# Gate products of three branches: one matmul of 512 columns for both parts of x, their halves added on the VectorE

## The reference

```python
h = rms_norm(h_res, pre_norm_g[i])            # 16 meta rows + 256 rows
z = h @ w_in[i]                               # the last 4096 columns are gl
y_a = (pool_mixer(pv, ...) * silu(pg)) @ w_out_pool[i]      # pool
y_b = (mla_attention(...) * silu(mg)) @ w_out_mla[i]        # mla
y_c = (conformer_conv(cu, ...) * silu(cg)) @ w_out_conf[i]  # conf
y_d = (short_conv(sbcx, ...) * silu(sg)) @ w_out_sc[i]      # sc
gts = sigmoid(gl + gate_bias[i]).reshape(b_, l_, 4, D_MODEL)
m = gts[:, :, 0] * y_a + gts[:, :, 1] * y_b + gts[:, :, 2] * y_c + gts[:, :, 3] * y_d
h_res = h_res + rms_norm(m @ w_o[i], post_norm_g[i])
```

## Time and profile before

| | |
|---|---|
| median of 3 runs | 875.02 us |
| the profiled execution | 877.89 us, its span 876.2 us |
| TensorE, matmuls | 863.1 us busy (99%), 5932 matmuls |
| VectorE | 588.7 us busy (67%) |
| ScalarE | 426.8 us busy (49%) |
| GpSimd | 86.8 us busy (10%) |
| HBM | 174 GB/s over the span |

### The profile page before, as it was taken

How to read it: one execution, slowest core, us unless ns; L and a number is a source line. 1 busy time by engine, 2 the same in 40 slices (tenths; PEclk the granted TensorE clock), 3 DMA queues, 4 the chain that set the end, 5 groups by cost and what they waited for, 6 DMA issues and landing times.

```text
span 876.2 us, 14097 instructions
## 1 busy us (share of the span) xinstructions
PE 863.1 (99%) x5932; PEld 795.3 (91%) x5932; DVE 588.7 (67%) x844; ACT 426.8 (49%) x614; POOL 86.8 (10%) x85
## 2 busy tenths in 40 slices
PE   8999999999999999999999999999999999999996
PEld 7998999999888988879999988889988899999885
DVE  4999956688586674786555554587987765555545
ACT  5656454456654873435444443255563554444320
POOL 0250100122003221011000000021100200000000
PEclk8999999999999999999999999999999999999999
DMA  9963776663356752547656656477544766565631
GB/s 288 246 182 101 192 212 175 176 184 121 97 168 185 239 159 91 157 153 243 187 177 190 191 185 198 125 244 223 162 142 131 237 185 192 177 185 192 188 125 49
DMA packets 121976, 154.51 MB, mean 176 GB/s; under 512 B 11647, under 2 KB 98074, under 8 KB 121914
## 3 DMA queue, kind: packets, MB, share of 16 engines
q1 hardware_dynamic: 120042, 148.36, 56.3%
q0 software_dynamic: 1872, 5.26, 2.0%
HBM read 151.48 MB, written 1.05 MB: 174 GB/s over the span
## 4 chain that ended last, share of the span: by engine, by line
PE 92%; DVE 4%; DMA 2%; ACT 1%; issue 1%; SPq 0%; DVEq 0%
PE acc L594 26%; PE acc L595 25%; PE acc L596 25%; PE acc L678 2%; PE acc L681 2%; PE acc L679 2%; PE acc L632 1%; DMA staged<-in_ffn_w_gu 1%; PE misc L762 1%; DMA x<-in_x 1%; DVE y L2108 1%; PE misc L819 1%; PE misc L1016 1%; ACT w_hi L1221 1%; DVE w_lo L1645 1%
## 5 line engine op out<-in xcount | busy, mean ns | idle before, releaser
L1645 DVE TENSOR_TENSOR w_lo<-staged,w_hi 128x1024 fp32r<-128x1024 f32 (+1 forms) x274 | 332.0, 1232 | 157.4 <-ACT w_hi L1221 156.5
L594 PE MATMUL acc<-x_hi,w_hi 128*128 128x256 f32 (+2 forms) x1288 | 365.8, 284 | 0.0
L595 PE MATMUL acc<-x_lo,w_hi 128*128 128x256 f32 (+2 forms) x1288 | 363.8, 282 | 0.0
L596 PE MATMUL acc<-x_hi,w_lo 128*128 128x256 f32 (+2 forms) x1288 | 361.2, 280 | 0.0
L1221 ACT CAST w_hi<-staged 128x1024 fp32r<-128x1024 f32 (+1 forms) x274 | 277.8, 1044 | 85.7 <-DMA staged<-in_ffn_w_down 44.6
L596 PEld LDWEIGHTS acc<-x_hi,w_lo 128*128 128x128 f32 x1288 | 243.7, 189 | 0.0
L594 PEld LDWEIGHTS acc<-x_hi,w_hi 128*128 128x128 f32 x1288 | 241.6, 188 | 1.7 <-issue 1.0
L595 PEld LDWEIGHTS acc<-x_lo,w_hi 128*128 128x128 f32 x1288 | 242.1, 188 | 0.7 <-issue 0.2
L594 PE MATMUL acc<-w_hi,h_hi 128*128 128x512 f32 (+1 forms) x176 | 66.4, 377 | 0.0
L595 PE MATMUL acc<-w_lo,h_hi 128*128 128x512 f32 (+1 forms) x176 | 66.4, 377 | 0.0
L596 PE MATMUL acc<-w_hi,h_lo 128*128 128x512 f32 (+1 forms) x176 | 66.2, 376 | 0.0
(11 more groups left out here) (394 smaller groups left out, 1149.5 us busy)
## 6 DMA issues: line engine op xcount, KB each, us to landing
staged<-in_ffn_w_gu SPq DMA_DIRECT2D x88, 512.0 KB, 3.6
staged<-in_w_in SPq DMA_DIRECT2D x58, 512.0 KB, 3.9
staged<-in_ffn_w_down SPq DMA_DIRECT2D x44, 512.0 KB, 3.5
staged<-in_gla_w_in SPq DMA_DIRECT2D x24, 512.0 KB, 3.7
staged<-in_moba_w_in SPq DMA_DIRECT2D x24, 512.0 KB, 3.9
staged<-in_w_o SPq DMA_DIRECT2D x8, 512.0 KB, 3.8
staged<-in_gla_w_out SPq DMA_DIRECT2D x8, 512.0 KB, 3.8
staged<-in_moba_w_out SPq DMA_DIRECT2D x8, 512.0 KB, 3.7
```

Of the source, the lines that this page charges most:

```text
L594: pe.matmul(dst, st_hi, mv_hi, start=start, stop=False)
L595: pe.matmul(dst, st_hi, mv_lo, start=False, stop=False)
L596: return pe.matmul(dst, st_lo, mv_hi, start=False, stop=stop)
L1645: nc.vector.tensor_tensor(lo, raw, hi, ALU.subtract).then_inc(split, 1)
```

## The change

For the gates of sc, pool and conf the two parts of x now lie in one tensor, and one matmul multiplies the high weights by both (256 columns of `x_hi`, then 256 of `x_lo`) into the whole of a bank; the low weights by `x_hi` add to its first half, as before in a matmul of 256 columns. A slot has 8 matmuls of 512 columns and 8 of 256. The VectorE adds the two halves of each bank by a `tensor_reduce` over a view in which they are innermost, writes `gates`, and frees the pair. The ScalarE waits for that and takes the sigmoids in place in SBUF. `gate_out` waits for them on a new semaphore, `gated`. The gates of mla are computed as before.

```diff
-        x_hi = place("x_hi", [KC, KEYS], F32R)
-        x_lo = place("x_lo", [KC, KEYS], F32R)
+        x_parts = place("x_parts", [2, KC, KEYS], F32R)
+        x_hi, x_lo = x_parts[:, 0], x_parts[:, 1]
...
+            def wide_slot(sl, p, half):
+                ready(sl)
+                hi = w_hi[:, sl.ring(), :].rearrange("p (c n) -> p c n", c=4)
+                lo = w_lo[:, sl.ring(), :].rearrange("p (c n) -> p c n", c=4)
+                for b in range(2):
+                    for c in range(4):
+                        k = half * 4 + c
+                        cols = slice(b * P, b * P + P)
+                        def with_both():
+                            return pe.matmul(acc[:, p, b, :].rearrange("p (s n) -> p s n", s=2), hi[:, c, cols],
+                                             x_parts[:, :, k, META:KEYS], start=k == 0, stop=k == KC - 1)
+                        def with_high():
+                            return pe.matmul(acc[:, p, b, 0:ROWS], lo[:, c, cols], x_hi[:, k, META:KEYS], start=False, stop=False)
+                        if k == 0:
+                            with_both()
+                            mm = with_high()
+                        else:
+                            with_high()
+                            mm = with_both()
+                mm.then_inc(weights_used, 1)
...
-            t_stage(FIRST["gate_sc"], 8, OUT["gate_sc0"], xm_hi, xm_lo)
+            wide_stage(FIRST["gate_sc"], 8, OUT["gate_sc0"])
...
-                t_stage(FIRST["gate_pool%d" % h], 4, OUT["gate_pool%d" % (2 * h)], xm_hi, xm_lo)
+                wide_gates("pool", h)
...
-                t_stage(FIRST["gate_conf%d" % h], 4, OUT["gate_conf%d" % (2 * h)], xm_hi, xm_lo)
+                wide_gates("conf", h)
...
             def take_gates(b, before, i):
-                name = "gate_%s%d" % (b, i)
-                if before:
-                    await_out(act, "y_%s%d" % (before, i))
-                nc.scalar.activation(gates[:, 2 * i, :], acc[:, pair(name), 0, 0:ROWS], ACT.Sigmoid,
-                                     bias=gate_bias(b, 2 * i))
-                copy_out(gates[:, 2 * i + 1, :], acc[:, pair(name), 1, 0:ROWS], name, ACT.Sigmoid,
-                         bias=gate_bias(b, 2 * i + 1))
+                await_out(act, "gate_%s%d" % (b, i))
+                for c in (2 * i, 2 * i + 1):
+                    last = nc.scalar.activation(gates[:, c, :], gates[:, c, :], ACT.Sigmoid, bias=gate_bias(b, c))
+                last.then_inc(s["gated"], 1)
...
             def gate_out(b, i):
                 name = "y_%s%d" % (b, i)
+                if b != "mla":
+                    dve.wait_ge(s["gated"], 4 * ("sc", "pool", "conf").index(b) + i + 1)
...
+            def gate_sum(stage, index):
+                name = ...
+                slot_done(dve, stage, index)
+                parts = acc[:, pair(name), :, :].rearrange("p b (s n) -> p b n s", s=2)
+                taken(nc.vector.tensor_reduce(halves(gates, int(name[-1])), parts, AX.X, ALU.add), name)
             for sl in slots(FIRST["gate_sc"], 8):
                 lead(sl)
+                if sl.index % 2 == 1:
+                    gate_sum("gate_sc", sl.index)
...
                     for sl in slots(FIRST[stage], 4):
                         lead(sl)
+                        if sl.index % 2 == 1:
+                            gate_sum(stage, sl.index)
```

More of the change, by code:

```diff
@@ L396, in hybrid_stack @@
             "cleared", "conf_rounded", "conf_sig", "conf_split", "conf_squared", "conf_u", "conf_zn", "const_loaded",
-            "conv_done", "cum_ready", "e_ready", "end_ready", "exp_done", "gain_loaded", "gain_scaled", "gg0_ready",
+            "conv_done", "cum_ready", "e_ready", "end_ready", "exp_done", "gain_loaded", "gated", "gain_scaled", "gg0_ready",
             "gg1_ready", "gk_loaded", "glu_ready", "h_rounded", "h_split", "half_ready", "heads_done", "intra_ready",
@@ L619, in t_stage, with wide_gates, wide_stage @@
                            first=sl.index % 2 == 0, last=sl.index % 2 == 1)
+            def wide_slot(sl, p, half):
[18 more added lines that the diff above has]
+                mm.then_inc(weights_used, 1)
+            def wide_gates(b, h):
+                for sl in slots(FIRST["gate_%s%d" % (b, h)], 4):
+                    name = "gate_%s%d" % (b, 2 * h + sl.index // 2)
+                    if sl.index % 2 == 0:
+                        open_out(name)
+                    wide_slot(sl, pair(name), sl.index % 2)
+            def wide_stage(first, count, out0):
+                for sl in slots(first, count):
+                    o = out0 + sl.index // 2
+                    if sl.index % 2 == 0:
+                        open_out(OUTS[o])
+                    wide_slot(sl, o % 2, sl.index % 2)
             def first_slots(turn):
@@ L1947, in take_out @@
                 gate_out(b, 2 * h + 1)
+            def gate_sum(stage, index):
+                name = "%s%d" % (stage[:-1], 2 * int(stage[-1]) + index // 2) if stage != "gate_sc" else "gate_sc%d" % (index // 2)
+                slot_done(dve, stage, index)
+                parts = acc[:, pair(name), :, :].rearrange("p b (s n) -> p b n s", s=2)
+                taken(nc.vector.tensor_reduce(halves(gates, int(name[-1])), parts, AX.X, ALU.add), name)
             for sl in slots(FIRST["gate_sc"], 8):
                 lead(sl)
+                if sl.index % 2 == 1:
+                    gate_sum("gate_sc", sl.index)
                 if sl.index == 0:
```

## The result

The changed kernel takes 886.85 us (median of 4 runs, 886.58 to 888.21), the kernel before beside it 874.78 us (median of 4, 874.51 to 878.23). The ratio is 1.0137, with a 95% interval of 1.0123 to 1.0151: 12.1 us slower, where 5.9 us were forecast. The sign and the places of the waits were right, the size was off by a factor of two: 886.85 lies above the forecast's own range (879 to 884) and inside the wide one, which reaches up to rival C.

The account below looks back on a forecast made before the run. The TensorE was taken to bound the kernel: 8.0 us of stalls less 2.1 us saved made it 5.9 us slower, from 875.02 to 880.9 us. Its own range was 879 to 884, the wide range 876.6 to 889.4.

Parts of the forecast that it names:

- rival C: Gate sums on the VectorE are slowed by their strided PSUM read to 1.97 us each: 889.4 us; chance 0.10.
- The saving: TensorE in 24 gate slots: 192 matmul pairs save 10.7 ns each, 2.1 us together; lower bound 0.8 us.
- The sum: VectorE in the gates: 12 added sums of 1024 values read a partition, 1.22 us each, or 1.14 in a list.
- B: Gate sums on the VectorE go at the pace of their outputs, 0.61 us each: 876.9 us; chance 0.13.
- The round of gate_sc: Two slots in gate_sc take 6.2 us from sum to last split; TensorE needs 5.5, VectorE falls 0.65 behind each round.
- The waits: TensorE stalls: y_sc1 2.0 us, y_sc3 and y_pool1 none, y_pool3 4.1, `conf_split` (y_conf0) 1.1, y_conf1 0.8; sum 8.0.
- The list of the VectorE from y_pool1 to the sum of gate_conf1: Before y_pool3: 12.8 us without idle, two sums of 1.14 and a 0.6 us cast wait; pair free at 181.5.
- rival D: Clock falls to 1.2 GHz in y_pool3's 4.1 us stall, some 7 us costing 3.4, 0.7 hidden: 883.6 us; chance 0.17.
- the prediction's own signs of being wrong: Reduction under 0.8 or over 1.5 us; no y_pool3 idle; clock under 1.00 at 175 to 195 us; distance over 240 ns.
- A (not slower): At the y outputs, the 6-slot lead and second pair absorb the sums; only shorter matmuls show: 873.0 us; chance 0.10.

Follow-up runs that it names:

- run 1: Changed kernel with the wide matmuls alone: no sums, no wait on `gated`, sigmoids from one half of each bank; 874.57 us, ratio 0.9991.
- table2: Changed kernel with a one-column sigmoid on the ScalarE behind the casts of the second gate slot, loading the table there; 883.12 us, ratio 1.0085.
- awake2: Changed kernel with unused matmuls in the TensorE's waits, 6 before y_sc1 and 9 before y_pool3; 883.96 us, ratio 1.0095.
- 6: Changed kernel with VectorE reordered: sums ahead of their slot's splits, last conf normalization behind y_pool3's product, conf low part ahead of its slot's split; 876.39 us.
- 7: Changed kernel with both the VectorE's new order and the ScalarE's sigmoids one lead later; 875.22 us, ratio 1.0006.
- 2: Changed kernel with the sums alone: old narrow matmuls, the VectorE's reduction reading one half twice; 885.84 us, ratio 1.0129.
- 5: Changed kernel with the ScalarE's sigmoids one lead later, behind the next casts, and the table loaded early; 878.49 us, ratio 1.0029.

## Why the prediction was right on the waits and wrong in its size

By the stretch, 5.9 us were forecast and 11.55 measured.

- **The saving.** Forecast 2.1 us, with 0.8 as the lower bound; measured 0.67 (run 1). In the changed kernel 9 pairs take 3.15 us (188.25 to 191.40), 350.0 ns each against three times 118.9 = 356.7: a pair saves 6.7 ns there, and 4.5 on the mean of gate_sc (0.29 us over 64 pairs). The matmul of 512 columns that follows one of 256 costs 350.0 - 118.9 = 231 ns, near the slower row and not the faster one that I took the earlier trace rows. 1.4 us of the error. The Trainium skill's formula ("TensorE: Matmul & The Clock Gate", Back-to-back issue gap) gave 0.5 us for the saving, and by the result that was the nearer value, though its distance for 256 columns (109 ns) is still not what the trace shows. The page gives the formula for single matmuls, and for a stream of weight loads and matmuls a sustained 131 ns at 512 columns; no run here shows that (227 to 234 ns).
- **The sum.** Forecast 1.22 us, measured 1.22 (twelve times). B (0.61) and C (1.97) fall. The operation reads two values 1 KB apart for each that it writes, and pays nothing for that against a split of 1024 values (1.22 us). It goes by values read. The Trainium skill ("VectorE: DVE Perf Modes", Side-by-side: where the cycles go for N=2048 bf16) counts by reads too, one per element at the 1x speed that Rules for kernel authors gives for `tensor_reduce`; the trace agrees.
- **The round of gate_sc.** Forecast 6.2 us, measured 6.25 and 6.24, but 7.53 in the first: I had left the table load out. Before, it stood in the ScalarE's idle time and no wait showed it. With it the first wait is 2.96 us, without it 1.68 (run table2); by distances, as the 2.0 forecast was worked out, 3.12 and 1.84. 1.1 us of the error.
- **The waits,** by distances of starts, as they were forecast, and at full clock (run awake2): at y_sc1 2.0 forecast and 3.12 measured; at y_sc3 and y_pool1 nothing, as forecast; at y_pool3 4.1 and 4.12; at y_conf0 1.1 and 1.41; at y_conf1 0.8 and 0.74. Together 9.4 us where 8.0 were forecast. The list of the VectorE from y_pool1 to the sum of gate_conf1, on which the largest one was worked out, holds.
- **The clock (rival D).** Priced at 2.7 us net with a chance of 0.17, and only in the wait at y_pool3. It fell in the wait at y_pool3 and behind that at y_sc1, and costs 2.8 us net (run awake2). With that one of the prediction's own signs of being wrong was met, a clock under 1.00 between 175 and 195 us (0.50 from 181.2 to 188.0). D should have been part of the forecast: the one fall that the trace of before has in its work comes after waits between matmuls too, and I had forecast such waits of 2.0 and 4.1 us. That its size came out is luck, since its errors cancel: the time behind y_pool3's wait loses 2.5 us and not 3.4, the one behind y_sc1's another 1.5 that I hadn't counted, and 1.3 of it are hidden where I had 0.7.
- **A (not slower)** falls: no lead absorbed the sums in the order that the change has. It is what runs 6 and 7 are, with another order.

The terms: 5.9 forecast + 1.4 (waits: 1.1 at y_sc1, mostly the table load, and 0.3 at y_conf0) + 1.4 (saving) + 2.8 (clock) = 11.5 us, against 11.55. Or from what was measured: waits of 9.4 us less the saving of 0.67 make 8.7, and awake2's stretch is 8.73 longer than before's; the clock adds 2.8. Why y_conf0 waits 0.3 us longer than forecast was not looked for. What I can't say from these runs is why the second low stretch was 6.8 us in after and 3.4 in runs 2, 5 and table2: the waits ahead of them were 3.95, 3.80, 3.19 and 3.95 us, so the length of the wait doesn't decide it alone.

## What to carry to other kernels

An added step in a chain that hands work from engine to engine (in gate_sc: sum, sigmoids, cast, split) has to be priced as a round against the bound engine's time for the same work, with everything that the chain's engines do once, a table load too, and not by how busy its engine is: with the VectorE 68% busy over the span there was no room. And an engine that runs its list in order has to be read up to the step that frees a buffer: here the largest wait came from work ahead of that step that could have stood behind it. Before a new operation is given up for its cost, try its place: here a few moved operations gave back ten of eleven and a half microseconds. And count a wait of several microseconds of the bound engine twice when the trace shows that its clock falls in or behind such waits.

## What the runs showed of the hardware that I had not expected

- In the midst of dense matmuls the granted clock fell to 1.2 GHz in or behind waits of 2.66, 2.80, 2.96, 3.19, 3.80 and 3.95 us, and not behind those of 1.68, 1.25 and 0.92 us. In the profiled execution of before it fell at about 13 us, among small matmuls, with no wait longer than 1.25 us ahead of it (9.98 to 11.23), so the length of one wait doesn't decide it alone.
- At the low level a matmul of 256 columns costs 0.213 us against 0.119, a factor of 1.8 and not 2: 0.213 us are 256 columns at 1.2 GHz with nothing on top, while at 2.4 GHz 12 ns stand on top of 107.
- The load of a table has no fixed place against the wait of the instruction that needs it: it stood ahead of the wait in the kernel before (in the ScalarE's idle time, at 111.63), behind the wait in the changed one (112.55), and took 1.28 us each time.
- Matmuls on plain float32 operands, of 256 columns, hold the TensorE for 0.413 us each, 3.5 times one of the kernel's own.
